# Attention head loop in full 128-row tiles, with the probabilities normalised on GpSimd

## The chip, the cores and the metric

The kernel runs on one core of one Trainium2 chip. The metric is device time in microseconds (us) for one execution of the whole program. Engines are called TensorE (PE in the profile; PEld is its weight load), VectorE (DVE), ScalarE (ACT), GpSimd (POOL) and SyncE (SP).

## The reference

Two blocks of two layers each run over 512 tokens of width 1024, in fp32. The first block (a gated linear recurrence, a pooling mixer, two dense MLPs) is not touched. Each layer of the second block is:

```
hn = rms_norm(x);  proj = hn @ w_in
out_a = neighbourhood_attention(q, k, v, rpb)   # 6 heads of 64; each 128-query tile sees 192 or 256 keys
out_b = mla_attention(q, k, v)                  # 6 heads, 96 wide, all 512 keys
out_c = short_conv_mixer(...)
mixed = concat(rms_norm(out_a), rms_norm(out_b), rms_norm(out_c))
x = x + mixed @ w_out
x = x + expert_choice_moe(rms_norm(x))          # 16 experts, top 64 tokens each, three 1024x1024 matrices per expert
# attention: softmax(q k^T * scale + bias) v ; softmax divides exp(s - max) by its row sum
```

## The kernel before

Everything lives in one SBUF arena; each engine has one program, written out by hand, and the engines meet at counting semaphores. Nothing is scheduled by a tool: the order of the code is the order of each engine's queue.

The part around the change is the head loop of the second block, once per layer (`for i in range(NU + 4)` on TensorE, with sister loops on VectorE and ScalarE). It has 36 units. A **unit of kind 0** is one 128-query tile t of the neighbourhood attention for two heads (h, h+1), and it is every third unit (i = 0, 3, 6, ...). A **unit of kind 1** is one 128-query tile of one latent (MLA) head against all 512 keys. Names: `qT`, `kT` hold queries and keys of two heads in 64 + 64 rows; `prob[i % 4]` holds the scores and then the probabilities of a unit; `probT` and `ptb` hold them transposed; `mixT` receives the head outputs.

For unit i, the steps are:

- TensorE `scores(i)` (iteration i). Kind 1 is one matmul, 96 rows by 512 columns (L2403). Kind 0 is two matmuls of 64 rows by 192 or 256 columns, one per head: the first at the start of the iteration (L2398), the second (`second_scores`, L2410) at its end, behind `turned` and `values` of older units.
- VectorE takes the maximum: for kind 0 it scales and adds the bias into `prob` (L1632, twice) and reduces (L1637); for kind 1 it reduces the PSUM bank (L1640) and scales one column (L1641).
- ScalarE takes the exponential with its row sum (L835 twice for kind 0, L838 for kind 1).
- VectorE, one iteration later and behind the maximum of unit i+1: the reciprocal of the sum (L1648), and then the product of the probabilities with it (L1651, twice for kind 0); this raises `p_done`.
- TensorE `turned(i)` (iteration i+3) transposes the 128x512 probabilities into PSUM (L2426 for kind 0, L2429 for kind 1), ScalarE copies them out (L855), and `values(i)` (iteration i+4) multiplies by v (L2449, L2456). For kind 0 with t = 0 or 3 only 192 keys count: `KEY_TILES` cuts the transposes and the value products into 128 and 64 rows, and for t = 0 half of the transposes are plain matmuls that write to the lower 64 rows.
- After the last unit of each pair of heads, ScalarE's `out_pair(n)` writes the outputs and their squares, and TensorE's `pair_sums(n)` (L2466, four small matmuls with `ones`) sums the squares into PSUM, n = 0 to 5. `added(7)` on VectorE reads these sums.

Behind the loop TensorE runs the 24 output projections `wout(n)` (L2483), mixed with the router, and then the experts. SyncE streams the expert weights, 96 loads of 2 MB per layer, in a fixed order through ten slots. The first loads wait for the stages that free their slots: slot 4 on `sc_done`, slot 3 on `o_ps`, slot 8 on `t_ps`, slots 7, 5, 0 on `wout_ps` 8, 16, 24 of the layer, slot 6 on the router's logits, slot 9 on saved rows. GpSimd is busy only with DMA issues and small copies.

## Time and profile before

| | before |
|---|---|
| three runs | 2665.82, 2668.63, 2669.02 us (median 2668.63) |
| span of the profiled execution | 2665.3 us |
| TensorE busy | 2554.9 us (96%) |
| VectorE / ScalarE / GpSimd busy | 1132.6 / 477.3 / 124.5 us |
| head loop, layer 0: TensorE starts at / the products `wout(2)` starts at | 1224.79 us / 1307.03 us |
| head loop, layer 1: starts at | 2023.24 us |

The profiled execution has no separate device time of its own on the page; its span is 0.5 us under the fastest of the three runs and 3.3 us under their median. A row of the timeline gives a start, a duration and a count of hardware passes: a fp32 matmul instruction is two passes, a transpose one. TensorE's durations overlap (each has its fill and drain in it), so the time that a step takes is read from the start of one row to the start of the next.

### The profile page before, as it was taken

The page shows a single profiled execution, that of the slowest core. Times are in us where ns is not written, and L with a number is a line of the kernel's source. Part 1 is how long each engine was busy: PE and PEld are TensorE (multiplying, and loading weights), DVE is VectorE, ACT ScalarE, POOL GpSimd, SP SyncE. Part 2 cuts the span into 40 slices and gives each one's busy share as a digit, 9 for nine tenths or more (in the row PEclk, how much of TensorE's full clock was granted, in tenths as well). Part 3 has the DMA queues.
Part 4 walks back from the last instruction along what each step waited for, and adds up shares of the span by engine and source line. Part 5 has one row for each costly group of instructions (what it writes and reads, how often), then busy time and mean ns, then how long its engine had stood idle before and what let it go on. Part 6 is the DMA issues. An engine that isn't in the chain of part 4 may idle for free.

```text
span 2665.3 us, 27166 instructions
## 1 busy us (share of the span) xinstructions
PE 2554.9 (96%) x11133; PEld 1545.6 (58%) x11133; DVE 1132.6 (42%) x1948; ACT 477.3 (18%) x1000; POOL 124.5 (5%) x233
## 2 busy tenths in 40 slices
PE   7999999999999999999999998889999999998888
PEld 3458888888888888465553333333455553333333
DVE  4765778645765645235541221113235541221112
ACT  2332121002222002125510000001125410000000
POOL 1320110000000000010000000000000000000000
PEclk9999999999999999999999999999999999999999
DMA  8632775451333244030349999999130349999998
GB/s 334 211 124 102 256 233 167 134 142 63 127 121 101 64 114 145 28 128 2 126 171 392 401 408 412 413 418 413 64 122 5 127 171 396 402 404 413 416 420 342
DMA packets 182730, 601.79 MB, mean 226 GB/s; under 512 B 8976, under 2 KB 123344, under 8 KB 157008
## 3 DMA queue, kind: packets, MB, share of 16 engines
q1 hardware_dynamic: 164544, 544.59, 53.7%
q0 software_dynamic: 16768, 51.22, 5.9%
q10 hardware_dynamic: 1296, 4.25, 0.4%
q8 instruction: 89, 1.46, 0.2%
q14 instruction: 33, 0.27, 0.0%
HBM read 593.74 MB, written 6.29 MB: 225 GB/s over the span
## 4 chain that ended last, share of the span: by engine, by line
PE 74%; DMA 20%; DVE 4%; SPq 1%; issue 1%; ACT 1%; DVEq 0%; ACTq 0%
DMA arena<-in_w_down 19%; PE ps L1997 10%; PE ps L2122 7%; PE ps L2571 7%; PE ps L2601 5%; PE ps L2008 5%; PE ps L2234 5%; PE ps L2483 4%; PE ps L1968 3%; PE ps L2228 3%; PE ps L1868 2%; PE ps L1917 2%; PE ps L2033 2%; PE ps L1892 2%; PE ps L2248 2%; PE ps L2403 2%
## 5 line engine op out<-in xcount | busy, mean ns | idle before, releaser
L2571 PE MATMUL ps<-arena 128*64 128x512 f32 x2048 | 452.2, 594 | 27.2 <-DMA arena<-in_w_up 25.5
L2571 PEld LDWEIGHTS ps<-arena 128*64 128x64 f32 x2048 | 147.1, 137 | 316.1 <-issue 263.7
L1997 PE MATMUL ps<-arena 128*128 128x256 f32 x1280 | 277.9, 379 | 2.0 <-issue 2.0
L1997 PEld LDWEIGHTS ps<-arena 128*128 128x128 f32 x1280 | 242.6, 190 | 35.8 <-issue 3.1
L2601 PE MATMUL ps<-arena 128*64 128x512 f32 x896 | 216.3, 640 | 41.5 <-DMA arena<-in_w_down 40.1
L2122 PE MATMUL ps<-arena 128*128 128x256 f32 x896 | 193.8, 379 | 0.2 <-DVE arena L1427 0.2
L2122 PEld LDWEIGHTS ps<-arena 128*128 128x128 f32 x896 | 170.1, 190 | 23.6 <-issue 0.5
L2601 PEld LDWEIGHTS ps<-arena 128*64 128x64 f32 x896 | 73.8, 148 | 181.7 <-issue 179.9
L2008 PE MATMUL ps<-arena 128*128 128x256 f32 x672 | 146.0, 379 | 0.0
L1778 DVE TENSOR_SCALAR arena<-ps,arena 128x512 f32<-128x512 f32 x32 | 22.7, 747 | 270.4 <-PE ps L2601 242.9
L2008 PEld LDWEIGHTS ps<-arena 128*128 128x128 f32 x672 | 127.5, 190 | 17.3
L2234 PE MATMUL ps<-arena 128*128 128x512 f32 x288 | 124.8, 593 | 0.0
L2614 PE MATMUL ps<-arena 128*128 128x512 f32 x256 | 120.4, 605 | 0.0
L1759 DVE SCALAR_TENSOR_TENSOR arena<-arena,ps 128x512 f32<-128x512 f32 x32 | 22.0, 688 | 221.8 <-ACT arena L885 221.8
L2483 PE MATMUL ps<-arena 128*128 128x512 f32 x256 | 115.3, 598 | 0.0
L885 ACT ACTIVATE arena<-ps 128x512 f32<-128x512 f32 x32 | 19.1, 598 | 529.8 <-PE ps L2571 529.8
L1968 PE MATMUL ps<-arena 128*128 128x256 f32 x512 | 112.6, 379 | 1.2 <-DVE arena L1154 1.2
L1761 DVE SCALAR_TENSOR_TENSOR arena<-arena,ps 128x512 f32<-128x512 f32 x32 | 22.0, 688 | 211.6 <-PE ps L2571 211.6
L1968 PEld LDWEIGHTS ps<-arena 128*128 128x128 f32 x512 | 97.0, 190 | 14.9 <-issue 1.9
L1753 DVE TENSOR_TENSOR arena<-ps,arena 128x512 f32<-128x512 f32 x128 | 88.5, 692 | 33.6 <-PE ps L2614 33.5
L942 DVE SCALAR_TENSOR_TENSOR arena<-arena,small 128x1024 f32<-128x1024 f32 x70 | 89.7, 1282 | 19.2 <-DMA arena<-in_w_mod 16.6
L2234 PEld LDWEIGHTS ps<-arena 128*128 128x128 f32 x288 | 54.4, 190 | 66.9 <-issue 66.6
(433 smaller groups left out, 3060.4 us busy)
## 6 DMA issues: line engine op xcount, KB each, us to landing
arena<-in_w_gate SPq DMA_DIRECT2D x64, 2048.0 KB, 44.1
arena<-in_w_up SPq DMA_DIRECT2D x64, 2048.0 KB, 39.0
arena<-in_w_down SPq DMA_DIRECT2D x56, 2048.0 KB, 38.2
arena<-in_ffn_w SPq DMA_DIRECT2D x24, 2048.0 KB, 9.1
arena<-in_w_mod POOLq DMA_DIRECT2D x80, 512.0 KB, 5.2
arena<-in_ffn_w SPq DMA_DIRECT2D x32, 1024.0 KB, 7.7
arena<-in_w_down SPq DMA_DIRECT2D x16, 1024.0 KB, 35.7
arena<-in_w_in SPq DMA_DIRECT2D x10, 1536.0 KB, 12.2
```

Of the source, the lines that this page charges most:

```text
L942: ins = V.scalar_tensor_tensor(acc, mod_in[i % 3], cond[:, k:k + 1], acc, mul, add)
L1753: V.tensor_tensor(x, ps[:, MO_BANK[n % 4], :], x, add).then_inc(sm["mo_added"], 1)
L1968: ins = mm(ps[:, 2 * (i % 2) + k // 4, 0:256], w[:, k, P * (i % 4):P * (i % 4) + P], hT[:, k, 0:256], start=(k % 4 == 0), stop=(k % 4 == 3))
L1997: ins = mm(ps[:, i % 6, 0:256], src[:, k, P * j:P * j + P], x[:, k, :], start=(k == 0), stop=(k == 3))
L2008: ins = mm(ps[:, F2A_BANK[n], 0:256], w[:, f, :], x[:, f, :], start=(f == 0), stop=(f == 15))
L2122: ins = mm(ps[:, bank, 0:256], w[:, f, :], x[:, f, :], start=(f == 0), stop=(f == 15))
L2228: ins = mm(out_ps, hnT[:, k, cols:cols + out_ps.shape[0]], w[:, k, :], start=(k == 0), stop=(k == KC - 1))
L2234: ins = mm(ps[:, bank, :], w[:, k, c0:c0 + P], hnT[:, k, :], start=(k == 0), stop=(k == KC - 1))
L2483: ins = mm(ps[:, OUT_BANK[n], :], mixT(k)[:, P * t:P * t + P], w[:, (k + 2) % 8 % 4, 512 * half:512 * half + 512], start=(k == ks[0]), sto ...
L2571: ins = mm(ps[CAP * half:CAP * half + CAP, bank, :], xsT[:, 4 * q + k, :], wv[:, k, 512 * half:512 * half + 512], start=(q == 0 and k == 0 ...
L2601: ins.append(mm(ps[CAP * par:CAP * par + CAP, YE_BANK[half], :], hT2[par][:, k, CAP * q:CAP * q + CAP], w[par][0][:, k, 512 * half:512 * h ...
L2614: mm(ps[:, MO_BANK[n % 4], :], oh[:, P * t:P * t + P], ye[half], start=True, stop=True).then_inc(sm["mo_ps"], 1)
```

## The change

The change has these parts, for both layers:

1. **Scores of kind 0**: both heads' matmuls are issued together, each over all 128 rows, against `kT` as it is. For that the queries are split: `qT` keeps the first head's rows with the others multiplied by zero, and `q_other` holds the second head's. GpSimd makes both (`split(p)`, two 128x512 multiplications, p = 0, 1, 2; p = 0 ahead of the loop, the others behind units 0 and 1).
2. **Transposes and value products of kind 0**: always four full 128x128 transposes and four products over 128 rows. For t = 0 and 3 the 64 unused columns of each head in `prob` are set to zero by a GpSimd memset (`blank`).
3. **Normalisation**: VectorE stops at the reciprocal (`p_inv`), GpSimd waits for it, multiplies, and raises `p_done`.
4. **Order of `values`**: those of kind 1 come one iteration later (i-5).
5. **Sums of squares**: GpSimd adds the squares of the three pairs (`add_square`), and TensorE's `pair_sums` runs twice per layer, behind `wout(6)` and `wout(8)`, in place of six times. VectorE's three-column reduction before `ainv` is gone.
6. GpSimd's table loads for layer 1 (17 DMA issues) move from ahead of the head loop of layer 0 to behind it. Some semaphores of the first block are merged, with the same waits.

```diff
+        sq_part = [kT[:, 0, :], qT[:, 0, :]]
+        q_other = [at(lo, 512) for lo in (43552, 41504, 42016)]
...
-        KEY_TILES = (((0, 64, 64), (64, 128, 0)), ((0, 128, 0), (128, 128, 0)), ((0, 128, 0), (128, 128, 0)), ((0, 128, 0), (128, 64, 0)))
+        KEY_AT = (64, 0, 0, 0)
+        BLANK = {0: 0, 3: 192}
... ScalarE
                 for i in range(NU + 5):
-                    if i - 5 in U_LAST:
+                    if i - 5 in (9, 21, 33, 35):
                         out_pair(U_LAST.index(i - 5))
+                    if i - 6 in (11, 23):
+                        out_pair(U_LAST.index(i - 6))
... VectorE
                         m = 2 - kind
-                        chain(V.reciprocal(st[:, 48 + 2 * c:48 + 2 * c + m], st[:, 40 + 2 * c:40 + 2 * c + m]))
-                        for hh in range(m):
-                            x = prob[j % 4] if kind else prob[j % 4][:, 256 * hh:256 * hh + KEYS[t][1]]
-                            ins = V.tensor_scalar(x, x, st[:, 48 + 2 * c + hh:49 + 2 * c + hh], None, mul)
-                        ins.then_inc(sm["p_done"], 1)
+                        V.reciprocal(st[:, 48 + 2 * c:48 + 2 * c + m], st[:, 40 + 2 * c:40 + 2 * c + m]).then_inc(sm["p_inv"], 1)
... TensorE
+                        pe.wait_ge(sm["q_split"], 3 * l + h // 2 + 1)
                         k0, n = KEYS[t]
-                        mm(ps[:, bank, 0:n], qT[0:HD, h // 2, P * t:P * t + P], kT[0:HD, h // 2, k0:k0 + n], start=True, stop=True) \
-                            .then_inc(sm["s_half"], 1)
+                        for hh, q in enumerate((qT[:, h // 2, :], q_other[h // 2])):
+                            ins = mm(ps[:, bank, 256 * hh:256 * hh + n], q[:, P * t:P * t + P], kT[:, h // 2, k0:k0 + n], start=True, stop=True)
+                        ins.then_inc(sm["s_ps"], 1)
...
-                    bank = 2 + i % 2
-                    if kind == 0:
-                        for hh in range(2):
-                            for kt, (lo, n, row) in enumerate(KEY_TILES[t]):
-                                dst, src = ps[row:row + n, bank, 256 * hh + P * kt:256 * hh + P * kt + P], prob[i % 4][:, 256 * hh + lo:256 * hh + lo + n]
-                                ins = mm(dst, src, ident, start=True, stop=True) if row else tr(dst, src, ident)
-                    else:
-                        for kt in range(TC):
-                            ins = tr(ps[:, bank, P * kt:P * kt + P], prob[i % 4][:, P * kt:P * kt + P], ident)
+                    for kt in range(TC):
+                        ins = tr(ps[:, 2 + i % 2, P * kt:P * kt + P], prob[i % 4][:, P * kt:P * kt + P], ident)
...
                     if 3 <= i < NU + 3:
                         turned(i - 3)
-                    if i >= 4 and i - 4 in O_VALUE:
+                    if i >= 5 and (i - 5) % 6 == 5:
+                        values(i - 5)
+                    if i >= 4 and ((i - 4) % 3 == 0 or i - 4 == NU - 1):
                         values(i - 4)
-                    if i < NU and UNITS[i][0] == 0:
-                        second_scores(i)
-                    if i - 7 in U_LAST[:4]:
-                        pair_sums(U_LAST.index(i - 7))
...
-                pair_sums(4)
-                wout(6)
-                pair_sums(5)
-                for n in range(7, 24):
+                for n in range(6, 24):
                     wout(n)
+                    if n in (6, 8):
+                        pair_sums(n // 2 - 3)
... GpSimd
+                def split(p):
+                    G.tensor_scalar(q_other[p], qT[:, p, :], const[:, C_HM + 1:C_HM + 2], None, ALU.mult)
+                    G.tensor_scalar(qT[:, p, :], qT[:, p, :], const[:, C_HM:C_HM + 1], None, ALU.mult).then_inc(sm["q_split"], 1)
+                pool.wait_ge(sm["q_copied"], 3 * l + 3)
+                pool.wait_ge(sm["st_T"], 15 * l + 3)
+                split(0)
+                pool.wait_ge(sm["st_T"], 15 * l + 15)
+                for i, (kind, h, t) in enumerate(UNITS):
+                    if i in BLANK_UNITS:
+                        blank(i)
+                    pool.wait_ge(sm["p_inv"], NU * l + i + 1)
+                    c = i % 4
+                    for hh in range(2 - kind):
+                        x = prob[c] if kind else prob[c][:, 256 * hh + KEY_AT[t]:256 * hh + KEY_AT[t] + KEYS[t][1]]
+                        ins = G.tensor_scalar(x, x, st[:, 48 + 2 * c + hh:49 + 2 * c + hh], None, ALU.mult)
+                    ins.then_inc(sm["p_done"], 1)
+                    if i in (0, 1):
+                        split(i + 1)
+                    if i in (26, 30):
+                        add_square(2 + (i == 30))
+                add_square(4)
+                add_square(5)
```

TensorE's queue in the middle of the loop, units 12 to 14 (t = 0, 192 keys), before the change. L2398 and L2410 are the two halves of the kind 0 scores, L2403 the kind 1 scores, L2426 and L2429 the transposes, L2449 the kind 0 values:

```order
L2398 MATMUL ps<-arena 128x192
L2426 MATMUL ps<-const,arena 128x128 x4
L2410 MATMUL ps<-arena 128x192
L2403 MATMUL ps<-arena 128x512
L2429 MATMUL ps<-const,arena 128x128 x4
L2449 MATMUL ps<-arena 64x128 x4
L2403 MATMUL ps<-arena 128x512
L2429 MATMUL ps<-const,arena 128x128 x4
```

The same units after the change, with L2401 the kind 0 scores, L2406 the kind 1 scores, L2417 all transposes and L2436 the kind 0 values:

```order
L2401 MATMUL ps<-arena 128x192 x2
L2417 MATMUL ps<-const,arena 128x128 x4
L2406 MATMUL ps<-arena 128x512
L2417 MATMUL ps<-const,arena 128x128 x4
L2436 MATMUL ps<-arena 64x128 x4
L2406 MATMUL ps<-arena 128x512
L2417 MATMUL ps<-const,arena 128x128 x4
```

The second half of the kind 0 scores has moved from behind the transposes to directly behind the first half, and one row is gone.

GpSimd's queue at the head loop of layer 0 after the change; before it, nothing of the head loop stood on this engine. L2696 and L2697 are `split`, L2704 is `blank`, L2725 the normalisation of units 0, 1, 2, 3 and so on:

```order
L2696 ISA
L2696 TENSOR_SCALAR arena<-arena,const 128x512
L2697 TENSOR_SCALAR arena<-arena,const 128x512
L2704 MEMSET arena 128x2x64
L2725 TENSOR_SCALAR arena<-arena,st 128x192 x2
L2696 TENSOR_SCALAR arena<-arena,const 128x512
L2697 TENSOR_SCALAR arena<-arena,const 128x512
L2725 TENSOR_SCALAR arena<-arena,st 128x512
L2696 TENSOR_SCALAR arena<-arena,const 128x512
L2697 TENSOR_SCALAR arena<-arena,const 128x512
L2725 TENSOR_SCALAR arena<-arena,st 128x512
L2725 TENSOR_SCALAR arena<-arena,st 128x256 x2
```

Two splits of two instructions each stand ahead of the normalisation of units 1 and 2.

## Rows read from the trace of the kernel before

**Rows 1.** Windows over both head loops (us, then busy us of each engine, PEclk, DMA share, GB/s):

```profile
1224.80:1318.80 94.00, 93.00 (x504) 52.34 (x504) 63.16 (x175) 60.00 (x147) 0.00 (x0) 1.00 0.08 28
2023.40:2117.40 94.00, 93.00 (x503) 52.26 (x504) 63.01 (x175) 59.96 (x147) 0.00 (x0) 1.00 0.09 29
```

**Rows 2.** TensorE's waits, 1224 to 1320 us, the only row:

```profile
PE ps L2426 <- DVE arena L1651: 0.9, 1, 0.9
```

**Rows 3.** Timeline of TensorE, units 15 to 17 (start, us, line, form, passes):

```profile
1256.34 0.70 PE L2398 MATMUL ps<-arena 64*128 64x256 f32 x2
1256.97 1.32 PE L2426 MATMUL ps<-const,arena 128*64 128x128 f32 x6
1258.21 1.95 PE L2456 MATMUL ps<-arena 128*64 128x256 f32 x16
1260.09 0.70 PE L2410 MATMUL ps<-arena 64*128 64x256 f32 x2
1260.72 1.12 PE L2403 MATMUL ps<-arena 96*128 96x512 f32 x2
1261.68 0.60 PE L2429 MATMUL ps<-const,arena 128*128 128x128 f32 x4
1262.21 0.80 PE L2449 MATMUL ps<-arena 64*64 64x128 f32 x8
1262.95 1.05 PE L2466 MATMUL ps<-ones,arena 128*128 128x1 f32 x8
1263.86 1.10 PE L2403 MATMUL ps<-arena 96*128 96x512 f32 x2
1264.80 0.60 PE L2429 MATMUL ps<-const,arena 128*128 128x128 f32 x4
1265.34 0.70 PE L2398 MATMUL ps<-arena 64*128 64x256 f32 x2
```

**Rows 4.** The same timeline, kind 0 values over full 128 rows:

```profile
1269.56 0.66 PE L2449 MATMUL ps<-arena 128*64 128x128 f32 x8
1270.15 1.12 PE L2403 MATMUL ps<-arena 96*128 96x512 f32 x2
```

**Rows 5.** The same timeline, full 128x128 shapes next to each other:

```profile
1307.03 1.88 PE L2483 MATMUL ps<-arena 128*128 128x512 f32 x4
1308.75 0.60 PE L2429 MATMUL ps<-const,arena 128*128 128x128 f32 x4
...
1311.83 0.60 PE L2429 MATMUL ps<-const,arena 128*128 128x128 f32 x4
1312.27 1.88 PE L2483 MATMUL ps<-arena 128*128 128x512 f32 x4
```

**Rows 6.** Timeline: first scores of unit 0 and of unit 3, last units' transposes:

```profile
1224.79 0.59 PE L2398 MATMUL ps<-arena 64*128 64x192 f32 x2
...
1231.30 0.70 PE L2398 MATMUL ps<-arena 64*128 64x256 f32 x2
...
1306.56 0.63 PE L2426 MATMUL ps<-const,arena 128*128 128x128 f32 x4
```

**Rows 7.** GpSimd's largest compute instruction, by groups:

```profile
L2660 POOL MEMSET tbl<- 120x480 f32 x1 | 0.5, 518 | 0.0
```

**Rows 8.** VectorE and ScalarE in the loop, groups by form (busy us, mean ns):

```profile
L838 ACT ACTIVATE arena<-ps,st,arena 128x512 f32<-128x512 f32 x24 | 18.7, 779 | 2.9 <-DVE st L1641 2.5
L1640 DVE TENSOR_REDUCE st<-ps 128x1 f32<-128x512 f32 x24 | 16.4, 685 | 1.4 <-PE ps L2403 1.4
L1632 DVE SCALAR_TENSOR_TENSOR arena<-ps,arena 128x256 f32<-128x256 f32 x12 | 5.3, 480 | 11.1 <-PE ps L2410 11.1
```

**Rows 9.** Timeline: the loop's first reciprocal:

```profile
1228.54 0.17 DVE L1648 RECIPROCAL st<-st 128x2 f32<-128x2 f32 x1 [0.20 <-ACT arena L835]
```

**Rows 10.** SyncE's queue behind the loop (start of the DMA issues):

```profile
1321.37 2.15 SPq L458 DMA_DIRECT2D arena<-in_w_gate  x2
1343.79 25.55 SPq L458 DMA_DIRECT2D arena<-in_w_up  x2
```

More of the change, by code:

```diff
@@ L324, in program @@
         O_VALUE = {i: n + 1 for n, i in enumerate(O_UNITS)}
+        BLANK_UNITS = [i for i in range(NU) if UNITS[i][0] == 0 and UNITS[i][2] in BLANK]
         IN_LANDS = (2, 2, 2, 1, 1, 1)
@@ L556, in gates @@
                 A(xr[:, c, 0:512], tmp[2 + j], ACT.Tanh, scale=small[:, 10, c:c + 1],
-                  bias=small[:, 10, c:c + 1]).then_inc(sm["lru_T"], 1)
+                  bias=small[:, 10, c:c + 1]).then_inc(sm["lru_root"], 1)
             def decay(c):
@@ L593, in _ @@
             for c in range(KC):
-                act.wait_ge(sm["lru_T"], c + 1)
-                A(xr[:, c, 0:512], xr[:, c, 0:512], ACT.Sqrt, bias=tiny[:, 0:1]).then_inc(sm["sqrt_done"], 1)
+                act.wait_ge(sm["lru_root"], c + 1)
+                A(xr[:, c, 0:512], xr[:, c, 0:512], ACT.Sqrt, bias=tiny[:, 0:1]).then_inc(sm["lru_root"], 1)
             for c in range(1, KC):
@@ L2710, in _, with blank, add_square @@
             for l in range(DEPTH):
+                def split(p):
+                    G.tensor_scalar(q_other[p], qT[:, p, :], const[:, C_HM + 1:C_HM + 2], None, ALU.mult)
+                    G.tensor_scalar(qT[:, p, :], qT[:, p, :], const[:, C_HM:C_HM + 1], None, ALU.mult).then_inc(sm["q_split"], 1)
+                def blank(i):
+                    if i >= 4:
+                        pool.wait_ge(sm["pt_ps"], NU * l + i - 3)
+                    lo = BLANK[UNITS[i][2]]
+                    G.memset(prob[i % 4].rearrange("p (h n) -> p h n", h=2)[:, :, lo:lo + HD], 0.0)
+                def add_square(n):
+                    kind = n % 2
+                    pool.wait_ge(sm["o_done"], 6 * l + n + 1)
+                    if n >= 4:
+                        pool.wait_ge(sm["sq_added"], 4 * l + n - 3)
+                    G.tensor_tensor(sqm[kind], sqm[kind], sq_part[kind], add).then_inc(sm["sq_added"], 1)
+                pool.wait_ge(sm["q_copied"], 3 * l + 3)
[17 more added lines that the diff above has]
+                add_square(5)
                 if l == 0:
-                    pool.wait_ge(sm["bias_ps"], 6)
                     pool.dma_start(flip, a["consts"][0:CAP, C_FLIP:C_FLIP + CAP]).then_inc(sm["tbl_in"], 16)
```

55 lines of the change are left out of this document (23 added, 32 removed).

## The prediction

> **What bounds the kernel now.** I read the busy time of both head loops first, then TensorE's waits in the first of them, then TensorE's timeline row by row. [rows 1] show the loop twice, alike within 0.2 us: TensorE is busy 93.0 of 94 us at a granted clock of 1.00 (its upper level, 2.4 GHz), VectorE 63.2, ScalarE 60.0, GpSimd not at all, and the DMA is nearly idle. [rows 2] say that TensorE waited once, 0.9 us, for the normalisation on VectorE. So this stage is TensorE's own time, and faster VectorE work buys only that 0.9 us. A busy TensorE is not one that streams, though. In [rows 5] four passes of 512 columns take 1.72 us from start to start, 0.43 each, and four 128-column transposes 0.44: between full 128-row shapes there is no gap. In [rows 3], shapes change and gaps appear, read as start to start less the streaming (0.215 us per 256-column pass): L2398 to the next row 0.63 for 0.43 (0.20), L2410 0.63 for 0.43 (0.20), L2403 0.96 for 0.86 (0.10), L2429 0.53 for 0.43 (0.10), L2456 1.88 for 1.71 (0.17), and the mixed transposes of t = 0 take 1.24 where four plain ones take 0.44. These gaps are what the change can remove.
>
> The Trainium skill, TensorEngine Tiling (Array Packing), Key Properties, says that a change of tiling mode drains TensorE. By that rule the gaps go wherever neighbours become equal in shape, and stay around the 96-row scores; the trace agrees with its 0.10 to 0.20 us at each change and none in [rows 5].
>
> **The change part by part.** One group is three units, and I rebuild it from these start-to-start times. With 256 keys: both kind 0 scores, four passes, 0.86 and no gap; transposes, with a gap ahead of the 96-row scores, 0.53; kind 1 scores 0.96; transposes 0.53; kind 0 values 0.59 [rows 4], now for every t, where [rows 3] show 0.74 for a cut one; kind 1 scores 0.96; transposes 0.44, with full scores behind them. That is 4.87 us. With 192 keys it is four passes of 0.054 less, 4.66. Every other group has the large values between transposes and small values of the same shape, 1.88 - 0.17 = 1.71 more.
>
> - Units 3 to 35 are 11 groups, 6 with 256 keys, 5 with 192, 5 with large values: 6 x 4.87 + 5 x 4.66 + 5 x 1.71 = 61.1 us. Now they take 1306.56 - 1231.30 = 75.3 us [rows 6]. The difference is 14.2 us: four sets of sums that leave the loop, 0.91 each by [rows 3], are 3.6; the stall of [rows 2] is 0.9; shape changes are the other 9.7.
> - The first three units, with two output products: 1231.30 - 1224.79 = 6.51 us now [rows 6]; 0.64 + 0.10 + 1.72 + 0.10 + 3.44 = 6.00 then. Gain 0.5.
> - The stall of 0.9 us has its cause in VectorE's queue: two `added` steps stand ahead of the maxima and the reciprocal of unit 3. They stay. I give the 0.9 back.
> - The last two sets of sums stay on TensorE. Behind `wout(6)` and `wout(8)` their inputs, two GpSimd additions, are long ready. I cost them at nothing.
> - GpSimd's price for one 128x512 multiplication, x, is the open number; no row has one. Below, [rows 7]: 480 columns written, nothing read, 0.518 us, so 0.55 for 512. Above, twice that, a read and a write in turn, 1.1. Neither end is nearer, so I take 0.8, and 0.45 for 256 columns.
> - Does the longer chain fit? I take the tightest unit, a kind 1 unit i in front of a kind 0 unit, from the start of its iteration. The iteration lasts 1.40, the next scores 0.86; then VectorE's two additions of the bias (0.48 each) and the reduction (about 0.69, as L1640) [rows 8] end at 3.9. Then come the reciprocal, 0.17 [rows 9], and GpSimd. `turned(i)` is due after iterations of 1.40, 1.39 and 2.08 and the 0.96 of scores: at 5.8. I set 0.4 aside for handoffs. That leaves 1.3 us for x; at 0.8 it is covered by 0.5, and a cover gone costs what x exceeds 1.3, in one unit of three.
> - At the loop's start the two splits stand ahead of units 1 and 2. The first reciprocal ends at 1228.7 [rows 9], a memset follows, and units 0, split, 1, split, 2 take 0.9 + 1.6 + 0.8 + 1.6 + 0.8 = 5.7: done at 1234.6. `turned(2)` is due at about 1235.1 (1230.8 + 1.39 + 2.08 and 0.86 of scores). With x = 1.1 it is 1.6 us late. I take half of that, 0.8, as lost.
> - ScalarE's 60 us [rows 1] do not change, and the window shrinks from 94 to 80: 75% busy, not a bound. VectorE loses work. The first split starts when the keys are transposed and may take several us before unit 0 needs it; the ISA row ahead of it stands behind the last modulation load, hundreds of us earlier. The 17 moved table loads are issued before the router wants them.
>
> Sum for a layer: 14.2 + 0.5 - 0.9 - 0.8 = 13.0 us, for two 26.0.
>
> The Trainium skill, GPSIMD Engine Reference, Engine selection, speaks against the change: elementwise work belongs on VectorE, GpSimd being about twice as slow with two inputs and near line rate with one. Its best case for 512 elements is 0.77 us. Its ratio of 1.96 on the 0.685 us of [rows 8] would make x an estimated 1.34: the start would lose about 3 us, the steady chain next to nothing, and the time would be near 2647. No row here shows which holds.
>
> Does the gain reach the end? Behind the loop SyncE's stream of expert weights matters, since experts later wait for it. Its gates are events of TensorE and VectorE in and behind the loop, so they come earlier with it. One moves against that: slot 8's gate, the last sums, goes from behind `wout(6)` to behind `wout(8)`, some 4.4 us (10 passes of 0.43). In [rows 10] that gate opened at 1321.4, and the gate two loads later at 1343.8; the two loads between have some 10 us to spare. It costs nothing.
>
> The profiled span of 2665.3 us is 3.3 under the median, within the runs' spread; the gain is a difference of spans, so 2668.6 - 26 = **2642.6**.
>
> **The rivals.**
>
> *The two engines get in each other's way.* VectorE's small instructions (a column scaled, the reciprocal) wait while a GpSimd instruction holds something both need. If each of two per unit waits half of 0.8, a unit's chain grows 0.8 against a cover of 0.5: 0.3 on the worst unit of three up to all, 0.15 to 0.3 on average, times 72 units, 11 to 22 us back. The time would be 2653 to 2662. For it: both work in the same SBUF tiles, at once. Against it: VectorE's wide one-input instructions, which pass over 512 columns faster than its reductions do, are the very ones that leave. The trace has GpSimd at 0 in the loop [rows 1] and cannot tell. The Trainium skill, SBUF — State Buffer, tells of a port pair that VectorE and GpSimd lock for a whole instruction; by it, only VectorE's two-port or two-input instructions would wait, and few are left.
>
> *Slower: GpSimd becomes the bound.* In a layer's loop GpSimd has 24x for kind 1, 24 of 0.55x for kind 0, 4x of splits, about 2.6x of additions: 44x. The loop from unit 0 to the end of 35 is now 81.8 us [rows 6]. At x = 1.86 the two are equal, and above it the kernel is slower: at x = 2.1, 92 us, 2 x 10.6 more, 2690. Between 1.3 and 1.86 the gain shrinks toward nothing. For it: a software engine with a per-row scalar operand, never seen here; against it: [rows 7], which x would have to exceed 3.4-fold.
>
> *The change doesn't do what it says.* The gaps may belong to the step from transposes to products, not to row counts. If the kind 0 scores keep a 0.10 gap behind them and 0.20 ahead of the 96-row scores, each group keeps 0.2 more: 2.2 us a layer, 2647. If all gaps but those of the mixed transposes stayed, the gain would be sums and stalls only, about 2 x 5: 2658.
>
> *No change.* Should the weight stream not follow (its gates earlier, its end not), the time stays at 2668. [rows 10] show gates that opened by progress, so little speaks for it.
>
> **How the numbers follow.** Forecast with its bounds (x from 0.55 to 1.34, gaps of 0 to 0.2 more a group), 2638 to 2650: 0.57. Part of the gain, by the engines in each other's way, x of 1.4 to 1.8 or gaps that stay, 2650 to 2663: 0.23. Within 0.2% (5.3 us, about what a measurement of this kernel can tell from no change): 0.08. Slower: 0.12. The range leaves out 0.12 of slower, most of no change and a little below: 2637 to 2663. Faster 0.80, same 0.08, slower 0.12.
>
> **What would show it.** In the changed kernel, first scores of unit 3 to the first transposes behind unit 35's scores in about 62 us, not 75; kind 0 scores to transposes with no gap; a 192-key group in 4.7 us; GpSimd's 128x512 multiplication near 0.8; TensorE's waits in the loop under 3 us, all at the start. Wrong would be: waits of TensorE for GpSimd's L2725 spread over the loop; VectorE's one-column instructions longer than now while GpSimd works; a 0.20 gap ahead of L2406.

## The result, and the profile after

| | before | after |
|---|---|---|
| median of 13 runs each | 2668.73 us | 2660.71 us |
| range | 2665.82 to 2672.53 | 2656.64 to 2666.57 |
| ratio, 95% interval | | 0.997 [0.9962, 0.9978] |
| span of the profiled execution | 2665.3 us | 2654.8 us |
| layer 0: first scores of unit 0 to `wout(2)` | 82.24 us | 78.53 us |
| layer 1: the same | 82.24 us | 77.36 us |

The kernel is faster by 8.0 us, 0.3%, a third of the forecast 26. The two loops together give 3.7 + 4.9 = 8.6 us, so the gain is made in the loops and almost all of it reaches the end. The question is why a loop gives 4 us where 13 were worked out.

The first section of the page, busy time by engine: TensorE is busy 27 us less, 2527.7 for 2554.9, and GpSimd 145 us more. The kernel's time fell by far less than TensorE's work: TensorE now waits.

```profile
PE 2527.7 (95%) x11057; PEld 1538.3 (58%) x11057; DVE 1098.2 (41%) x1850; ACT 477.9 (18%) x1000; POOL 269.2 (10%) x361
```

TensorE's waits of after, in layer 0's loop (1220 to 1330 us), which answer to [rows 2]: the total, the number of waits, the longest.

```profile
PE ps L2417 <- POOL arena L2725: 7.9, 13, 1.7
```

Before, TensorE waited once, 0.9 us, for VectorE. Layer 1 of after shows 7.4 us in 14 waits. L2417 is the transposes, L2725 the multiplication on GpSimd.

The windows of layer 0's loop of after, which answer to [rows 1]: units 0 to 2, the next 12.8 us, the rest up to `wout(2)`. Behind the duration stands the busy time of TensorE, its weight load, VectorE, ScalarE and GpSimd, then the granted clock.

```profile
1221.70:1227.51 5.81, 5.81 (x19) 2.93 (x18) 3.60 (x10) 4.59 (x11) 2.42 (x4) 1.00 0.00 0
1227.51:1240.33 12.82, 9.88 (x40) 5.88 (x38) 6.06 (x15) 5.00 (x12) 11.89 (x9) 0.73 0.01 2
1240.33:1300.23 59.90, 55.13 (x356) 34.56 (x354) 33.23 (x96) 44.22 (x115) 49.21 (x46) 1.00 0.10 36
```

Units 0 to 2 take 5.81 us, for 6.51 before and 6.00 forecast. In the second window GpSimd is busy 11.9 of 12.8 us, TensorE 9.9, at a granted clock of 0.73. In the third GpSimd has a sixth of its time free, yet TensorE is idle for 4.8 us.

Groups of after by form, 1215 to 1320 us: busy time and mean ns of one, then the idle time before them.

```profile
L2725 POOL TENSOR_SCALAR arena<-arena,st 128x512 f32<-128x512 f32 x24 | 37.5, 1567 | 12.0 <-DVE st L1653 12.0
L2725 POOL TENSOR_SCALAR arena<-arena,st 128x256 f32<-128x256 f32 x12 | 11.0, 927 | 0.0
...
L2712 POOL TENSOR_TENSOR arena<-arena 128x512 f32<-128x512 f32 x4 | 5.1, 1273 | 5.8 <-ACT arena L826 5.8
L1646 DVE TENSOR_SCALAR st<-st,arena 128x1 f32<-128x1 f32 x24 | 5.1, 214 | 0.8
L1653 DVE RECIPROCAL st<-st 128x1 f32<-128x1 f32 x24 | 3.7, 155 | 0.9 <-ACT arena L844 0.9
```

This is the number that no row of before had. GpSimd's 128x512 multiplication takes 1.57 us, where I had taken 0.8, between 0.55 and 1.1; that of 256 columns takes 0.93, where I had taken 0.45. The Trainium skill, GPSIMD Engine Reference, Engine selection, calls one-input work "roughly line-rate", and the page's best case for 512 elements is 0.77 us: the trace disagrees, the instruction takes twice that. The addition of two tiles (L2712) is the cheaper one, 1.27 us.

**Where the waits fall in the steady loop.** Timeline of TensorE, after, one 192-key group (start, duration, passes, in brackets the idle time ahead of the row and its releaser):

```profile
1250.12 0.82 PE L2401 MATMUL ps<-arena 128*128 128x192 f32 x4
1250.78 0.60 PE L2417 MATMUL ps<-const,arena 128*128 128x128 f32 x4
1251.21 1.02 PE L2406 MATMUL ps<-arena 96*128 96x512 f32 x2
1252.70 0.63 PE L2417 MATMUL ps<-const,arena 128*128 128x128 f32 x4 [0.46 <-POOL arena L2725]
...
1254.81 0.60 PE L2417 MATMUL ps<-const,arena 128*128 128x128 f32 x4
1255.24 1.03 PE L2401 MATMUL ps<-arena 128*128 128x256 f32 x4
```

The full-shape scores run into the transposes with no gap (0.66 for 4 x 0.16, then 0.43), as forecast. The group begins with unit 12, so the next transposes are those of unit 10, `turned(10)` in iteration 13: the kind 1 unit directly behind a kind 0 unit. They wait 0.46 us. From unit 9 on the timeline has such a wait in every group of three units: 0.46 (once 0.52) in a group with 192 keys, 0.25 in one with 256, which is 0.21 longer. The chain of all engines that leads to the wait above, same kernel:

```profile
1249.88 0.69 DVE L1645 TENSOR_REDUCE st<-ps 128x1 f32<-128x512 f32 x1 [3.04 <-PE ps L2406]
...
1250.74 0.15 DVE L1653 RECIPROCAL st<-st 128x1 f32<-128x1 f32 x1
...
1250.99 3.11 POOL L2725 TENSOR_SCALAR arena<-arena,st 128x512 f32<-128x512 f32 x2 [2.11 <-DVE st L1653]
```

GpSimd was idle for 2.11 us when the reciprocal of unit 10 came at 1250.89. Its instruction ran from 1250.99 to about 1252.55, and TensorE started at 1252.70. An engine with time to spare is still late, since one instruction of it is long. The second product of that row is unit 11's, the kind 1 unit in front of the next kind 0 unit. It ends at 1254.10, 0.7 us before its transposes at 1254.81.

In the groups that begin with units 9, 21 and 33 (192 keys too) the wait stands one step earlier, ahead of the transposes of a kind 0 unit. The two products of that unit stand in GpSimd's queue directly behind a kind 1 product. Here is GpSimd with units 29 and 30, three instructions in 3.37 us, then TensorE at the transposes of unit 30:

```profile
1289.22 3.37 POOL L2725 TENSOR_SCALAR arena<-arena,st 128x512 f32<-128x512 f32 x3 [0.48 <-DVE st L1653]
...
1292.74 0.63 PE L2417 MATMUL ps<-const,arena 128*128 128x128 f32 x4 [0.46 <-POOL arena L2725]
```

**The start of the loop.** GpSimd of after, where the splits (L2696, L2697) stand between the first products:

```profile
1226.78 1.56 POOL L2696 TENSOR_SCALAR arena<-arena,const 128x512 f32<-128x512 f32 x1
...
1229.86 1.57 POOL L2725 TENSOR_SCALAR arena<-arena,st 128x512 f32<-128x512 f32 x1
```

Units 0 and 1 are each followed by such a pair: a split takes 3.1 us in place of 1.6. TensorE over the same stretch, in windows of 2 us (TensorE's busy time, then the clock):

```profile
1230.00:1232.00 2.00, 0.42 (x4) 1.00 0.00 0
1232.00:1234.00 2.00, 2.00 (x12) 0.61 0.06 12
1234.00:1236.00 2.00, 1.00 (x2) 0.50 0.00 0
...
1240.00:1242.00 2.00, 2.00 (x16) 1.00 0.00 0
```

TensorE waits 1.74 us (up to 1231.58) and 1.20 us (up to 1236.20). Between them the granted clock falls from its upper level, 2.4 GHz, to 0.50, which is 1.2 GHz, and it comes back at about 1239.2. In windows of 0.5 us it stands at 0.50 for some 6.8 us, the second wait among them, and in layer 1 for some 3.4 us.

### The profile page after: what moved, and what is told of

It reads as the page before. It is cut to its first block, busy times and chain, and to the rows that moved or that the text cites. A ratio compares the mean times of both kernels' runs of the same rounds, so it can differ in the third digit from the quotient of the medians.

```text
span 2654.8 us, 27052 instructions
## 1 busy us (share of the span) xinstructions
PE 2527.7 (95%) x11057; PEld 1538.3 (58%) x11057; DVE 1098.2 (41%) x1850; ACT 477.9 (18%) x1000; POOL 269.2 (10%) x361
## 4 chain that ended last, share of the span: by engine, by line
PE 72%; DMA 19%; DVE 4%; POOL 2%; SPq 1%; issue 1%; ACT 1%; DVEq 0%; ACTq 0%
DMA arena<-in_w_down 18%; PE ps L1998 10%; PE ps L2554 8%; PE ps L2123 7%; PE ps L2584 6%; PE ps L2009 5%; PE ps L2235 5%; PE ps L2469 4%; PE ps L1969 3%; PE ps L2229 3%; PE ps L1869 2%; PE ps L1918 2%; PE ps L2034 2%; PE ps L1893 2%; POOL arena L2725 2%; PE ps L2249 2%
## 5 line engine op out<-in xcount | busy, mean ns | idle before, releaser
L1998 PEld LDWEIGHTS ps<-arena 128*128 128x128 f32 x1280 | 242.6, 190 | 35.8 <-issue 3.1
L2123 PEld LDWEIGHTS ps<-arena 128*128 128x128 f32 x896 | 170.1, 190 | 23.6 <-issue 0.5
L2009 PEld LDWEIGHTS ps<-arena 128*128 128x128 f32 x672 | 127.5, 190 | 17.3
L2725 POOL TENSOR_SCALAR arena<-arena,st 128x512 f32<-128x512 f32 (+2 forms) x96 | 114.6, 1208 | 29.2 <-DVE st L1653 29.0
L2696 POOL TENSOR_SCALAR arena<-arena,const 128x512 f32<-128x512 f32 x6 | 9.4, 1568 | 963.4 <-PE ps L2381 963.4
L1969 PEld LDWEIGHTS ps<-arena 128*128 128x128 f32 x512 | 97.0, 190 | 14.9 <-issue 1.9
```

Source lines behind the costliest of these rows:

```text
L1969: ins = mm(ps[:, 2 * (i % 2) + k // 4, 0:256], w[:, k, P * (i % 4):P * (i % 4) + P], hT[:, k, 0:256], start=(k % 4 == 0), stop=(k % 4 == 3))
L1998: ins = mm(ps[:, i % 6, 0:256], src[:, k, P * j:P * j + P], x[:, k, :], start=(k == 0), stop=(k == 3))
L2009: ins = mm(ps[:, F2A_BANK[n], 0:256], w[:, f, :], x[:, f, :], start=(f == 0), stop=(f == 15))
L2123: ins = mm(ps[:, bank, 0:256], w[:, f, :], x[:, f, :], start=(f == 0), stop=(f == 15))
L2725: ins = G.tensor_scalar(x, x, st[:, 48 + 2 * c + hh:49 + 2 * c + hh], None, ALU.mult)
```

## The experiments

All are timed in five rounds against the kernel before on the same chip; the ratio is to that. "Loop" is from unit 0's scores to `wout(2)`, layer 0, layer 1.

| kernel | median us (range) | ratio [95%] | loops us |
|---|---|---|---|
| after, for comparison | 2660.71 (2656.64 to 2666.57) | 0.9970 [0.9962, 0.9978] | 78.53, 77.36 |
| norm_vector | 2641.38 (2640.22 to 2644.01) | 0.9903 [0.9887, 0.9918] | 67.83, 67.82 |
| norm_gpsimd_only | 2681.51 (2677.80 to 2686.64) | 1.0058 [1.0045, 1.0072] | 88.37, 88.71 |
| sums_only | 2665.36 (2662.57 to 2668.47) | 0.9987 [0.9978, 0.9996] | 79.03, 79.03 |
| splits_vector | 2655.96 (2654.65 to 2660.17) | 0.9957 [0.9943, 0.9970] | 73.87, 73.88 |
| stall_filled | 2662.59 (2657.82 to 2666.54) | 0.9977 [0.9968, 0.9986] | 78.65, 78.64 |
| kind0_vector | 2653.14 (2651.31 to 2654.70) | 0.9944 [0.9931, 0.9958] | 73.05, 73.06 |
| kind1_vector | 2648.41 (2644.37 to 2653.64) | 0.9929 [0.9916, 0.9943] | 72.12, 72.11 |
| norm_tt | 2639.06 (2636.24 to 2647.12) | 0.9906 [0.9893, 0.9920] | 68.40, 68.40 |
| product_tt | 2647.81 (2647.26 to 2651.45) | 0.9927 [0.9913, 0.9940] | 70.43, 72.11 |
| old_shapes_tt | 2671.05 (2668.61 to 2678.89) | 1.0018 [1.0007, 1.0029] | 82.77, 82.77 |
| full_scores_tt | 2642.18 (2641.15 to 2644.57) | 0.9903 [0.9888, 0.9918] | 68.39, 68.38 |
| full_scores | 2643.49 (2639.26 to 2644.81) | 0.9901 [0.9886, 0.9917] | 67.78, 67.78 |

### The parts apart: is it the shapes or the product?

**norm_vector**: after, with the product back on VectorE; GpSimd keeps the blanks, the splits (both behind unit 0's blank) and the additions.

```diff
-                        V.reciprocal(...).then_inc(sm["p_inv"], 1)
+                        chain(V.reciprocal(...))
+                        for hh in range(m):
+                            ins = V.tensor_scalar(x, x, st[:, 48 + 2 * c + hh:49 + 2 * c + hh], None, mul)
+                        ins.then_inc(sm["p_done"], 1)
```

> The changed kernel with the product of probabilities and reciprocal back on VectorE; all else of the change stays, and GpSimd makes the three splits, the zeroed columns and the added squares. Theory A (GpSimd's 1.57 us product is too slow for the shorter loop, and the full shapes are worth what was forecast): units 3 to 35 take 61 to 64 us instead of 71.8, no half-clock stretch, time 2641 to 2647. Theory B (the shape change itself gives little at the end, because the weight stream or VectorE's queue takes it back): the loop gets short but the time stays at 2655 to 2661, or the loop stays above 68 us with waits for VectorE.

Measured: 2641.38 us, faster than before by 27. TensorE's waits in the loop, 1222 to 1292 us:

```profile
PE ps L2442 <- ACT arena L861: 0.8, 2, 0.4
PE ps L2423 <- DVE arena L1656: 0.7, 2, 0.6
```

The same 192-key group as above, in this kernel:

```profile
1244.51 0.82 PE L2405 MATMUL ps<-arena 128*128 128x192 f32 x4
1245.16 0.60 PE L2423 MATMUL ps<-const,arena 128*128 128x128 f32 x4
1245.59 1.02 PE L2410 MATMUL ps<-arena 96*128 96x512 f32 x2
1246.46 0.60 PE L2423 MATMUL ps<-const,arena 128*128 128x128 f32 x4
...
1247.58 1.12 PE L2410 MATMUL ps<-arena 96*128 96x512 f32 x2
1248.54 0.60 PE L2423 MATMUL ps<-const,arena 128*128 128x128 f32 x4
1248.98 1.03 PE L2405 MATMUL ps<-arena 128*128 128x256 f32 x4
```

The group takes 4.47 us, where 4.66 was forecast: the row into the 96-row scores takes 0.43 and the scores 0.87, with no gap on either side. Only behind the values (128x64) do they take 0.96. In after the group takes 5.12: its wait of 0.46 costs 0.65. Part of the rest is overlap that is lost: the scores' row ahead of the wait lasts its full 1.02 us, where the next row otherwise starts 0.87 behind its start. So the changes of shape and order are worth about what was forecast (parts 1, 2 and 4 were not run apart), and the product on GpSimd, with the splits in its queue, takes 19 of the 27 us back.

**norm_gpsimd_only**: before, with only the product moved to GpSimd, in the same form as in after (the merged semaphores of part 6 are in it too, as in sums_only and old_shapes_tt).

```diff
 VectorE
-                        chain(V.reciprocal(...))
-                        for hh in range(m):
-                            ins = V.tensor_scalar(x, x, ...)
-                        ins.then_inc(sm["p_done"], 1)
+                        V.reciprocal(...).then_inc(sm["p_inv"], 1)
 GpSimd
+                for i, (kind, h, t) in enumerate(UNITS):
+                    pool.wait_ge(sm["p_inv"], NU * l + i + 1)
+                    for hh in range(2 - kind):
+                        ins = G.tensor_scalar(x, x, st[:, 48 + 2 * c + hh:49 + 2 * c + hh], None, ALU.mult)
+                    ins.then_inc(sm["p_done"], 1)
```

> The kernel before with only the product moved to GpSimd (old shapes, old order, six sets of sums). Theory A: GpSimd needs 5.0 us a group where TensorE takes 6.8 on average and 5.4 in the shortest, so TensorE waits only in the first groups; loop 76 to 78 us, time 2669 to 2674. Theory B (GpSimd and VectorE hold each other up): VectorE's one-column instructions grow and the loop takes over 80 us, time over 2678.

Measured: 2681.51 us, slower than before by 13. The loop and the time are those of theory B, but its cause is not there: VectorE's one-column scaling takes 214 ns and its one-column reciprocal 155, as before. The loop waits 5.1 us for GpSimd, nearly all of it at kind 0 transposes:

```profile
PE ps L2422 <- POOL arena L2712: 4.5, 9, 1.2
```

TensorE, VectorE and GpSimd of this kernel, in time's order:

```profile
1273.17 0.63 PE L2422 MATMUL ps<-const,arena 128*128 128x128 f32 x4 [0.32 <-POOL arena L2712]
...
1275.61 0.59 PE L2406 MATMUL ps<-arena 64*128 64x192 f32 x2
...
1276.23 0.74 DVE L1632 SCALAR_TENSOR_TENSOR arena<-ps,arena 128x192 f32<-128x192 f32 x2 [3.29 <-PE ps L2406]
...
1277.48 0.15 DVE L1648 RECIPROCAL st<-st 128x1 f32<-128x1 f32 x1
...
1277.73 4.58 POOL L2712 TENSOR_SCALAR arena<-arena,st 128x512 f32<-128x512 f32 x4 [3.13 <-DVE st L1648]
```

In the old order these rows hand the lateness on. The transposes wait for GpSimd; `second_scores` (L2406) stands behind them; its result is what the maximum on VectorE waits for; and the reciprocal of the older kind 1 unit stands behind that maximum, so GpSimd gets it late again, and the product of the kind 0 unit stands behind that one. By the order of the code the change's part 1, both scores issued at the start, cuts this circle; no run has part 1 alone.

**sums_only**: before, with the additions on GpSimd and two sets of sums in place of six.

```diff
-                pair_sums(4)
-                wout(6)
-                pair_sums(5)
-                for n in range(7, 24):
+                for n in range(6, 24):
                     wout(n)
+                    if n in (6, 8):
+                        pair_sums(n // 2 - 3)
 GpSimd
+                for n in range(2, 6):
+                    add_square(n)
```

> The kernel before with only the squares added on GpSimd and two sets of sums in place of six. Theory A: four sets of 0.91 us leave each loop, 7.3 us in all, time 2661 to 2662. Theory B (they fill time that TensorE loses anyway, or the later gate of slot 8 costs): 2665 to 2670.

Measured: 2665.36 us. Each loop is 3.21 us shorter, against 3.6 in the sum; of these 6.4 us the time shows about 3 (by the ratio's interval 1.1 to 5.9).

### The start of the loop: queue and clock

**splits_vector**: after, with splits 1 and 2 on VectorE, where they are needed only from unit 12 on.

```diff
 VectorE, at the start of iteration i
+                    if i in (7, 10):
+                        p = 1 + (i == 10)
+                        V.tensor_scalar(q_other[p], qT[:, p, :], ..., None, mul)
+                        V.tensor_scalar(qT[:, p, :], qT[:, p, :], ..., None, mul).then_inc(sm["q_split"], 1)
 GpSimd
-                    if i in (0, 1):
-                        split(i + 1)
```

> The changed kernel with the splits of pairs 1 and 2 on VectorE, behind units 7 and 10. GpSimd loses 6.3 us of work at the start of each loop. Theory A: the 3.5 us of waits in units 1 to 6 and the half-clock stretch behind them go to under 1 us, the waits of 0.25 to 0.46 in the short groups stay; 4 to 6 us less per layer, time 2649 to 2653. Theory B (the start would stall anyway on VectorE's two added steps, the clock falls anyway): 2657 to 2661.

Measured: 2655.96 us, above the 2649 to 2653 of theory A: of the 8.1 us that the two loops lose against after, the time shows 4 to 5. The loops are 4.7 and 3.5 us shorter than in after. In layer 0, 7.9 - 5.6 = 2.3 are waits:

```profile
PE ps L2421 <- POOL arena L2729: 5.6, 12, 1.3
```

The granted clock is 1.00 from the loop's start on. So the splits in GpSimd's queue cost about 4 us a layer, in layer 0 about half of it by the waits and half by the clock. What is left are the waits of 0.46 and 0.25 of the steady loop; one of 1.29 (unit 31), for whose product GpSimd stood behind an addition; and one of 0.99 at the transposes of unit 3, whose reciprocal stands behind VectorE's two `added` steps.

**stall_filled**: after, with five matmuls of no use ahead of the waits in units 1, 2 and 3, so that TensorE isn't idle while it waits.

```diff
+                    if i in (1, 2, 3):
+                        for _ in range(5):
+                            mm(ps[:, 2 + i % 2, 0:256], ident, const[:, C_ID:C_ID + 256], start=True, stop=True)
                     pe.wait_ge(sm["p_done"], NU * l + i + 1)
```

> The changed kernel, with five extra 128x128x256 matmuls (10 passes of 0.215 us, 2.2 us) ahead of TensorE's wait for the product in units 1, 2 and 3 of each loop; their result is overwritten by the transposes. It adds 6.5 us of TensorE work per layer where 3.5 us are waited away. Theory A (the idle time at the start makes the clock fall, and the half-clock stretch costs over 2 us per layer): the granted clock stays at 1.00, the loop takes 78.5 to 79.5 us, no more than now, as what it adds beyond the waits (about 3) is won back at the clock. Theory B (the clock falls for another reason, or costs nothing): clock falls as before and the loop grows by 3 us or more, to 81 or 82 us.

Measured: TensorE's windows over the start of both loops:

```profile
1220.00:1240.00 20.00, 20.00 (x102) 1.00 0.00 1
2015.00:2035.00 20.00, 20.00 (x103) 1.00 0.00 1
```

The clock stays at 1.00. The loops take 78.65 and 78.64 us, 0.1 and 1.3 more than in after, and the time is not told apart from it. What the clock gives back, the added matmuls take. So without the idle time there the clock doesn't fall, but this is no repair. That the same idle time always makes it fall is not so, as product_tt shows below.

### The steady loop: rate or length of the chain?

**kind0_vector**: splits_vector, with the products and blanks of kind 0 on VectorE. GpSimd has only the 24 products of kind 1 left.

```diff
+                        if kind:
+                            V.reciprocal(...).then_inc(sm["p_inv"], 1)
+                        else:
+                            chain(V.reciprocal(...))
+                            for hh in range(2):
+                                ins = V.tensor_scalar(x, x, st[:, 48 + 2 * c + hh:49 + 2 * c + hh], None, mul)
+                            ins.then_inc(sm["p_inv"], 1)
```

> The changed kernel with splits 1 and 2, the zeroed columns and the kind 0 products on VectorE; GpSimd keeps the kind 1 products, 1.57 us each, 3.1 us a group where TensorE takes 4.66 at least. Theory A (rate: GpSimd is full in the short groups): TensorE waits for GpSimd under 1 us in a loop, loop 68 to 69 us, time 2642 to 2645. Theory B (chain: 1.57 us is over the 1.3 us that a kind 1 unit's chain leaves): waits of about 0.3 us in each of 12 groups remain, loop 71 to 73 us, time 2649 to 2654.

Measured: 2653.14 us, waits of 5.4 us a loop. TensorE's timeline:

```profile
1252.47 0.63 PE L2430 MATMUL ps<-const,arena 128*128 128x128 f32 x4 [0.46 <-POOL arena L2735]
...
1257.60 0.63 PE L2430 MATMUL ps<-const,arena 128*128 128x128 f32 x4 [0.25 <-POOL arena L2735]
```

And GpSimd's group, 1225 to 1299 us:

```profile
L2735 POOL TENSOR_SCALAR arena<-arena,st 128x512 f32<-128x512 f32 x22 | 34.5, 1572 | 34.5 <-DVE st L1656 34.5
```

GpSimd has now half of its time free, all of it waiting for the reciprocal, and the waits of 0.46 and 0.25 at these kind 1 transposes stand as they were. There it is the length of the chain of one unit, not GpSimd's load. The load has a small part: in the group of unit 21 the wait moves from the kind 0 transposes to the kind 1 transposes behind them, and the group takes 6.84 us for 7.09 in after, where norm_vector has 6.20.

**kind1_vector**: the reverse, products of kind 1 on VectorE, those of kind 0 on GpSimd; in the code above `if kind` becomes `if kind == 0`.

> The changed kernel with splits 1 and 2 and the kind 1 products on VectorE; GpSimd keeps the kind 0 products (0.93 or 0.77 us each, two a unit) and the zeroed columns, under 2.1 us a group. Theory A (rate): no waits for GpSimd, loop 68 to 69 us, time 2642 to 2645. Theory B (chain): the kind 0 chain with 1.9 us on GpSimd is near its due time as well, single waits of 0.1 to 0.3 us, loop 69 to 71 us.

Measured: 2648.41 us. Two of TensorE's five waits for GpSimd in layer 0's loop:

```profile
1237.36 0.63 PE L2425 MATMUL ps<-const,arena 128*128 128x128 f32 x4 [1.92 <-POOL arena L2734]
...
1266.72 0.63 PE L2425 MATMUL ps<-const,arena 128*128 128x128 f32 x4 [0.41 <-POOL arena L2734]
```

The wait in every group is gone. Four of 0.29 and 0.41 are left in the steady loop, 1.4 us, at the transposes of kind 0 units with their two products, and one of 1.92 at those of unit 3: its reciprocal stands behind the two `added` steps, and GpSimd's two products follow. The clock over 1220 to 1240 us is 0.95, and in layer 1, over 2015 to 2035 us, 0.91; so the loop of 72.12 us is above the 69 to 71 of theory B. The chain that was late in every group was that of the kind 1 units.

### The price of the instruction

**norm_tt**: splits_vector, with the product in another form: two tensors, the second the reciprocal broadcast along the row.

```diff
-                        ins = G.tensor_scalar(x, x, st[:, 48 + 2 * c + hh:49 + 2 * c + hh], None, ALU.mult)
+                        ins = G.tensor_tensor(x, x, st[:, 48 + 2 * c + hh:49 + 2 * c + hh].to_broadcast([P, x.shape[1]]), ALU.mult)
```

> The changed kernel with splits 1 and 2 on VectorE, and GpSimd's product written as a two-tensor multiplication by the broadcast reciprocal. GpSimd's two-tensor addition of 128x512 took 1.27 us in the changed kernel, its multiplication by a per-row scalar 1.57. Theory A (rate): at 1.27 and about 0.65 to 0.8 a half, a group needs 4.0 us, under 4.66, the waits in the short groups go, loop 68 to 70 us instead of 73.9, time 2644 to 2648. Theory B (broadcast costs as much as the scalar, 1.57 or more): loop 73.9 us or more, time 2656 or more.

Measured: 2639.06 us, the lowest median of all, though not told apart from norm_vector. Its products for kind 1, 1225 to 1290 us, then TensorE in the group of unit 12:

```profile
L2729 POOL TENSOR_TENSOR arena<-arena,st 128x512 f32<-128x512 f32 x22 | 22.8, 1040 | 20.0 <-DVE st L1653 20.0
...
1246.00 1.02 PE L2410 MATMUL ps<-arena 96*128 96x512 f32 x2
1246.94 0.63 PE L2421 MATMUL ps<-const,arena 128*128 128x128 f32 x4
```

One product takes 1.04 us in place of 1.57, and of the waits for GpSimd one remains, 0.65, that behind an addition. (Three short ones for ScalarE's copies, 0.65, 0.39 and 0.39, are there too.) 5.5 us a loop come from this line. It is still a little late in a 192-key group: the transposes start 0.94 us behind the scores, not 0.87, and the group takes 4.58 us for 4.47 in norm_vector. With 256 keys nothing is lost, 6.41 for 6.41.

**product_tt** and **old_shapes_tt**: the same line alone, in after and in norm_gpsimd_only.

> The changed kernel with one thing altered: GpSimd's product as a two-tensor multiplication by the broadcast reciprocal, which took 1.04 us for 512 columns where the product by a per-row scalar took 1.57. All splits stay on GpSimd at 1.57 us each. Theory A (the forecast failed only in this price): the waits of 0.25 to 0.46 us a group go, 1 to 2.5 us of waits at the start stay, loop 69 to 72 us instead of 78, time 2641 to 2648. Theory B (the splits ahead of units 1 and 2 matter as much as the price): waits at the start over 3 us and a fall of the clock, loop over 73 us, time over 2650.

> The kernel before with only the product on GpSimd, in the two-tensor form of 1.04 us. With the form of 1.57 us this kernel was slower by 13 us, a loop of 88.4 us against 82.2. Theory A (each unit's chain is longer than VectorE's way by the product's price, and what is over its cover shows as waits): the excess falls by about 0.5 us a unit, most waits go, loop 82 to 84 us, time 2667 to 2672. Theory B (handing over to a third engine costs by itself): loop 86 us or more, time 2676 or more.

Measured: product_tt 2647.81 us, some 12 less than after by the two ratios. Three waits for GpSimd are left in layer 0, 3.1 us, two of them behind the splits. The longest of the three, and a window of 2 us behind its like in layer 1 (the clock is the third number from the end):

```profile
1236.80 0.63 PE L2417 MATMUL ps<-const,arena 128*128 128x128 f32 x4 [1.82 <-POOL arena L2725]
...
2027.00:2029.00 2.00, 2.00 (x8) 1.53 (x7) 0.00 (x0) 1.36 (x3) 1.40 (x2) 0.50 0.01 4
```

Both layers have these waits, 0.67 and 1.82 us. In layer 0 the clock stays at 1.00 behind them, in layer 1 it falls to 0.50 for some 3.4 us, and that loop is 1.7 us longer (72.11 for 70.43).

old_shapes_tt 2671.05 us, 0.2% slower than before: with a product of 1.04 us the circle of the old order all but goes, and its loop is 82.77 us beside 82.24 of before, for 88.37 with 1.57. So the price decides in the old order too.

### Which shapes make a gap?

**full_scores** (norm_vector) and **full_scores_tt** (norm_tt): the kind 1 scores over 128 rows, with rows 96 to 127 set to zero ahead of the loop.

```diff
-mm(ps[:, bank, :], qTb[0:QK, h, P * t:P * t + P], kTb[0:QK, h, :], ...)
+mm(ps[:, bank, :], qTb[:, h, P * t:P * t + P], kTb[:, h, :], ...)
```

> The same 128-row kind 1 scores with the product on VectorE (and the splits on GpSimd, where it has time). Theory A: loop 67.8 - 4.7 = 63 to 65 us, time 2631 to 2636. Theory B (VectorE, with 4.9 us of work in a group of 4.3, becomes the bound of the short groups): waits for VectorE of 0.3 us or more a short group, loop 65 to 67 us, time 2636 to 2640.

> The best kernel so far (product in the two-tensor form, splits 1 and 2 on VectorE) with the kind 1 scores over 128 rows as well; GpSimd zeroes the 32 unused rows of the keys and queries ahead of the loop. Every shape but that of the values is then equal. Theory A (a gap belongs to a step between row counts): four gaps of 0.10 us a group go, loop 68.4 - 4.7 = 63.7 us, up to 65 with waits, time 2629 to 2634. Theory B (the kind 1 gaps belong to something else, or the chain has no cover left in a group of 4.3 us): loop 67 us or more, time 2637 or more.

Measured: loops of 67.78 for 67.83, and 68.39 for 68.40. Nothing is gained, and the expected gap was not there to gain. Timeline of TensorE, full_scores_tt:

```profile
1252.62 1.02 PE L2410 MATMUL ps<-arena 128*128 128x512 f32 x2
1253.48 0.60 PE L2421 MATMUL ps<-const,arena 128*128 128x128 f32 x4
...
1256.32 1.13 PE L2410 MATMUL ps<-arena 128*128 128x512 f32 x2
1257.29 0.60 PE L2421 MATMUL ps<-const,arena 128*128 128x128 f32 x4
```

Scores over 128 rows take 0.86 between full tiles, and 0.97 behind values; those over 96 rows take 0.87 and 0.96 in norm_vector. The gap goes with the values, whose tile is 64 columns wide, and not with the 96 rows.

## Why the prediction was right in sign and wrong in size

**Shapes (9.7 us a layer, with the first units 0.5): right.** From norm_vector the loop gains 14.4 us a layer without the product on GpSimd, against 14.2 + 0.5 - 0.9 = 13.8. One error is to the good: I left 0.10 on each side of the 96-row scores, as [rows 3] seemed to say. There each of them stands behind a 64-row tile or the narrow sums; between full tiles it has no gap. The Trainium skill, TensorEngine Tiling (Array Packing), Key Properties, has a drain when the tiling mode changes. The trace agrees for the 64-row and 64-column shapes (0.09 to 0.20 us each), and shows 96 and 128 rows to be alike.

**Sums (3.6): 3.2** by sums_only. **The stall of 0.9**: in norm_vector the waits for VectorE are 0.7 and for ScalarE 0.8, so giving it back was about right.

**The failed step: "Neither end is nearer, so I take 0.8."** The bounds 0.55 and 1.1 of x came from one memset of [rows 7], with a read added as if it cost what a write does. x is 1.57, outside them. The kernel's shortfall hangs on that one number, in two terms of the sum:

- "A cover gone costs what x exceeds 1.3, in one unit of three." One unit of three was right, but it was the wrong unit. "I take the tightest unit, a kind 1 unit i in front of a kind 0 unit": that unit was not late. In after the product of unit 11 ends 0.7 us ahead of its transposes, most of it owed to the wait just before; in norm_tt it ends 0.8 ahead with no such wait. The one that waits is the other kind 1 unit, behind a kind 0 unit. Its cover, estimated as 1.57 less what the product costs its group, is 0.92 with 192 keys (5.12 us for 4.47 in norm_vector) and 1.13 with 256 (6.85 for 6.41), not 1.3. That the wait of 0.25 looks like my excess of 0.27 is chance: it costs 0.44. (In the groups of units 18 and 30 it costs nothing, 5.15 us in both kernels, as norm_vector waits 0.40 for ScalarE there.) At the x of 0.8 that I took, this unit would have been covered too, so the wrong unit alone would not have moved the sum. From splits_vector to norm_tt, where the steps differ only in the product's form (1.57 and 1.04), all this is 5.5 us a layer, where the sum had nothing. It holds part of the one wait of 1.29 behind an addition, which the sum had left out.
- "I take half of that, 0.8, as lost" for the splits at the start: 4.7 and 3.5 us by splits_vector. The queue is twice as long with x at 1.57, and about 2.4 us in layer 0 (rows at 0.50 against the same rows at 1.00) come from the clock, which I had as 1.00 throughout.

These close the account of layer 0: from unit 3's scores to `wout(2)`, after takes 72.72 us and norm_vector 62.03. Group by group, the first (9.57 for 4.69 us) loses 4.9, the next nine 3.7, and the last one with its tail (8.77 for 6.64) 2.1: 10.7 in all.

**The rivals.** "GpSimd becomes the bound" had its break-even at x = 1.86 by rate; after stands at 1.57, where that rival has the gain shrink, but the mechanism is in the main not the rate, by kind0_vector. The break-even was reckoned against the old loop of 81.8 us. Against the 67.8 of norm_vector the same 44x gives 1.54, so at 1.57 the rate would have been the next limit. "The engines get in each other's way" gave the time that came (2653 to 2662), and is not the cause: VectorE's one-column instructions take 0.214 and 0.155 us in after and 0.214 and 0.153 in norm_vector, where GpSimd is idle most of the time, and its reductions (0.684 and 0.685) and bias additions (0.479 and 0.478 for 256 columns) are alike too. "No change", by a weight stream that doesn't follow, is refuted: in norm_vector the loops give 28.8 us and the time 27.

The sign and the range held, since the range reached to 2663 for x between 1.4 and 1.8. The signs named beforehand came true in the half that says "wrong": waits for L2725 spread over the loop.

**Open**: sums_only showed about 3 us of the 6.4 of its loops, and splits_vector 4 to 5 of 8.1. Between the runs of a kernel lie 3 to 10 us, so where the rest went, if anywhere, can't be said. Nor was the wait of 0.65 behind an addition taken away in norm_tt. Why the same waits take the clock down in one layer of product_tt and not in the other stays open.

## What to carry to other kernels

Moving an operation to an idle engine changes two things: the load of the engines and the length of each unit's chain. Busy shares speak of the first alone, so count the time from one unit's first step to its last against the time until it is due, with the new engine's price in it. If that price has no row, find it before the rest of the sum (here one line in another form, 1.04 us for 1.57, was worth some 12 us). Work the chain out for every kind of unit, since the tightest need not be the one with the most steps. And when matmuls of several shapes alternate, read start to start between neighbours: here the padding of 64-row tiles to 128 went with the gaps, and that of 96 rows to 128 gained nothing.

## What the runs showed of the hardware that I had not expected

- GpSimd, 128x512 fp32: multiplication by a scalar of each row 1.57 us, addition of two tiles 1.27, multiplication by a broadcast column 1.04. The form with the fewest operands read is the slowest.
- Wide one-input instructions of both engines grow when they overlap. VectorE's 256 columns take 351 ns in norm_vector and 531 in kind0_vector, whose group (1225 to 1299 us) is the row below. GpSimd's take 927 in after and 967 in kind1_vector. These are means over instructions that overlap in part.

```profile
L1661 DVE TENSOR_SCALAR arena<-arena,st 128x256 f32<-128x256 f32 x12 | 5.9, 531 | 0.2
```

- The Trainium skill, SBUF — State Buffer, tells of a port pair which one of the two engines holds for a whole instruction. The trace agrees in kind: the wide one-input instructions grow, and VectorE's one-column instructions and its reductions and bias additions from PSUM don't.
- Behind one wait of 1.74 us the granted clock of after fell from 1.00 to 0.50, in layer 0 for some 6.8 us with a second wait of 1.20 in them (0.73 over 13 us), in layer 1 for some 3.4. One wait of 1.92 took it down in both layers of kind1_vector; waits of 0.67 and 1.82 took it down in one layer of product_tt and not in the other. The steady loop, with a wait of 0.25 or 0.46 in each group, kept 1.00.
